# Order of the scores, the second halves' turns and the exponentials in the two loops of sparse attention pairs

## The reference

```
s = q @ k.T * 0.125           # 512 x 512, only keys up to the query count
s = where(mask, s, -1e30)
p = softmax(s)                # NSA: times its gate
y = p @ v
```

## Time and profile before

| | |
|---|---|
| device time, three runs | 2798.03, 2798.65, 2803.75 us, median 2798.65 |
| the profiled execution's own time | 2803.71 us |
| its span in the profile | 2801.9 us |
| busy: PE, DVE, ACT, POOL | 2664.3 us (95%), 1644.3 us (59%), 1143.0 us (41%), 117.6 us (4%) |
| mean granted clock of TensorE | 0.985 |
| DSA's loop of pairs | about 1419 to 1498 us of the span |
| NSA's loop of pairs | about 1680 to 1831 us of the span |

### The profile page before, as it was taken

The page is one execution under the profiler, slowest core; times in us unless marked ns, Lnnn a source line. Parts: engine busy times, 40 slices in busy tenths (PEclk is TensorE's granted clock), DMA queues, the critical chain, the costliest instruction groups (busy, mean ns, idle before and its releaser), DMA issues.

```text
span 2801.9 us, 38810 instructions
## 1 busy us (share of the span) xinstructions
PE 2664.3 (95%) x13931; PEld 2138.0 (76%) x13931; DVE 1644.3 (59%) x3050; ACT 1143.0 (41%) x1988; POOL 117.6 (4%) x104
## 2 busy tenths in 40 slices
PE   7999999999999999999979988999999989999998
PEld 5567888888887888887856875577777768788887
DVE  6235725547876844637874267755677775563551
ACT  4444322236764322225364318822455552332221
POOL 0000000000000000001300010000111110000000
PEclk9999999999999999999999989999999999999999
DMA  4112333322222233332201310022222213433331
GB/s 143 46 54 67 105 98 97 99 83 68 75 81 77 76 105 97 98 98 83 76 16 46 99 38 1 1 83 83 83 68 68 68 53 98 129 91 103 90 101 64
DMA packets 59684, 217.82 MB, mean 78 GB/s; under 512 B 6432, under 2 KB 6560, under 8 KB 59424
## 3 DMA queue, kind: packets, MB, share of 16 engines
q1 hardware_dynamic: 57920, 209.76, 24.5%
q0 software_dynamic: 1632, 6.29, 0.7%
HBM read 211.83 MB, written 4.19 MB: 77 GB/s over the span
## 4 chain that ended last, share of the span: by engine, by line
PE 75%; DVE 13%; DVEq 4%; ACT 4%; issue 3%; ACTq 0%; DMA 0%; POOL 0%; SPq 0%
PE ps L385 21%; PE ps L387 21%; PE ps L386 21%; DVE work L2141 1%; PE ps L526 1%; DVE ring_lo L325 1%; DVE big L3377 1%; PE ps L777 1%; DVEq L3435 1%; DVE work L2160 1%; DVE work L2484 1%; PE ps L2066 1%; DVEq L2487 1%; DVE ps L2475 1%; ACT ring_hi L318 1%
## 5 line engine op out<-in xcount | busy, mean ns | idle before, releaser
L385 PE MATMUL ps<-a_hi,ring_hi 128*128 128x512 f32 (+1 forms) x1896 | 750.6, 396 | 34.9 <-DVE ring_lo L325 19.4
L387 PE MATMUL ps<-a_hi,ring_lo 128*128 128x512 f32 (+1 forms) x1912 | 742.0, 388 | 0.0
L325 DVE TENSOR_TENSOR ring_lo<-ring,ring_hi 128x1024 fp32r<-128x1024 f32 x358 | 437.8, 1224 | 484.4 <-ACT ring_hi L318 454.4
L386 PE MATMUL ps<-a_lo,ring_hi 128*128 128x512 f32 (+1 forms) x1832 | 710.8, 388 | 0.0
L318 ACT ACTIVATE ring_hi<-ring 128x1024 fp32r<-128x1024 f32 x376 | 395.5, 1055 | 498.4 <-PE ps L387 498.3
L385 PEld LDWEIGHTS ps<-a_hi,ring_hi 128*128 128x128 f32 x1896 | 358.5, 189 | 122.3 <-DVE ring_lo L325 18.3
L387 PEld LDWEIGHTS ps<-a_hi,ring_lo 128*128 128x128 f32 x1912 | 361.1, 189 | 74.9
L386 PEld LDWEIGHTS ps<-a_lo,ring_hi 128*128 128x128 f32 x1832 | 346.1, 189 | 68.4 <-issue 1.0
L386 PE MATMUL ps<-hid_lo,ring_hi 128*128 128x512 f32 (+1 forms) x992 | 380.6, 384 | 0.0
L385 PE MATMUL ps<-hid_hi,ring_hi 128*128 128x512 f32 (+1 forms) x928 | 354.6, 382 | 0.0
L387 PE MATMUL ps<-hid_hi,ring_lo 128*128 128x512 f32 (+1 forms) x928 | 354.2, 382 | 0.0
(11 more groups left out here) (450 smaller groups left out, 3343.2 us busy)
## 6 DMA issues: line engine op xcount, KB each, us to landing
ring<-weights SPq DMA_DIRECT2D x392, 512.0 KB, 3.6
h<-x SPq DMA_DIRECT2D x1, 2048.0 KB, 9.2
residual<-h POOLq DMA_DIRECT2D x4, 512.0 KB, 3.4
h<-residual POOLq DMA_DIRECT2D x1, 2048.0 KB, 11.4
out<-h POOLq DMA_DIRECT2D x1, 2048.0 KB, 7.9
tab<-tables SPq DMA_DIRECT2D x1, 1648.0 KB, 15.4
big<-positions SPq DMA_DIRECT2D x1, 256.0 KB, 3.4
col<-columns SPq DMA_DIRECT2D x1, 164.5 KB, 4.1
```

The source lines that it names most:

```text
L325: dve.tensor_tensor(lo, M.ring[:, b % RING, :], hi.bitcast(F32), ALU.subtract).then_inc(M.sem("blocks_split"), 1)
L385: pe.matmul(out, w_hi, hi, start=start, stop=False)
L386: pe.matmul(out, w_hi, lo, start=False, stop=False)
L387: return pe.matmul(out, w_lo, hi, start=False, stop=stop)
```

## The change

Three orders are changed, each by moving one step, and one wait is added so that no buffer is written before it is read. The work of each engine is the same.

```diff
@@ pe, body
                 turn(i, n, 0)
                 if n or not isinstance(i, int) or i:
                     out(i, n - 1)
-                turn(i, n, 1)
                 if n + 2 < per or nxt:
                     scores(i, n + 2)
+                turn(i, n, 1)
@@ act, body
                 keep(i, n, 0)
                 if n + 1 < per or nxt:
                     exp(i, n + 1, 0)
-                keep(i, n, 1)
                 if n or not isinstance(i, int) or i:
                     finish(i, n - 1)
                 if n + 1 < per or nxt:
                     exp(i, n + 1, 1)
+                keep(i, n, 1)
@@ dve, mask
-            dve.wait_ge(M.sem(f"{A}_scores"), i * per + (n + 1))
+            if half == 0 or (isinstance(i, int) and i == 0 and n < 2):
+                dve.wait_ge(M.sem(f"{A}_scores"), i * per + (n + 1))
+            else:
+                dve.wait_ge(M.sem(f"{A}_turned"), i * (6 * per) + 6 * (n - 1))
```

## The result

The new order is slightly slower (by 0.2%): median 2804.78 us (2802.62 to 2810.07, 10 runs) against 2798.47 (2797.34 to 2803.75, 10 runs) beside it, ratio 1.0022 with a 95% interval of 1.0012 to 1.0032, which is 3.4 to 9.0 us. The forecast's +4.6 lies in it; the bound of 0.2% (5.6 us) does too, so the measurement doesn't decide between the forecast's band, "within 0.2%", and "slower by more".

The account below looks back on a forecast made before the run. No engine had slack: TensorE was busiest, ScalarE nearly as tight, the chain through VectorE third. 0.8 + 1.96 - 0.5 + 0.5 + 1.8 = +4.6 us on the median 2798.65 gave 2803.3; range 2796.5 to 2811.

Parts of the forecast that it names:

- the forecast's band: Whole kernel: slower by +1.5 to +5.6 us; chance 0.36.
- Start, 0: Start of each loop: S(2) and S(3) stay where they were, 0 us; TensorE owes one turn.
- these prices: Both ends of both loops: slowdowns from TensorE's lower clock stay unchanged, as waits are of similar or greater length.
- Steady, +0.8 and +0.5: Steady steps: neighbouring turns and keeps add +0.20 four times in DSA, +0.09 six times in NSA.
- ScalarE's round of 8.35: Steady step: ScalarE's work sums to 8.35, more than TensorE's 8.22, so ScalarE sets the step.
- End, +1.96 and +1.8: Loop ends: T1(6) and T1(14) wait for a ScalarE copy; O(6) +1.96 in DSA, X +1.8 in NSA.
- The gain of O(7): End of DSA: O(7) no longer waits for F(6), only for the late K1(7); -0.5 us.
- The added wait, 0: VectorE's new wait before M1(n): T1(n-2) ends before M1(n) starts, so it costs 0.
- A: Steady steps: neighbouring turns let TensorE's clock fall, 48 us in some 22 steps, 2851; chance 0.04.
- B: Steady steps: if M1 comes late, E1, K1, both turns and out slide; 2806 to 2812; chance 0.32.
- C: Turns: waits for the first copy partly go in neighbouring turns, 10 us off, 2793; chance 0.12.
- D: The lower clock falls into the new idle time and costs less; up to -6 us, 2797; chance 0.16.

Follow-up runs that it names:

- e3: Changed kernel, but ScalarE keeps the old order in each loop's last step with an exponential; 2805.89 us, 1.0024 of the kernel before.
- e7: Changed kernel with one more 128x512 copy on ScalarE ahead of each finish of DSA; 2813.49 us, one execution.
- e8: Kernel before with one more 128x512 copy on ScalarE ahead of each finish of DSA; 2805.55 us, one execution.
- e1: Changed kernel, but step 0 of each loop keeps the old order on TensorE and ScalarE; 2801.10 us, 1.0009 of the kernel before.
- e4: Changed kernel with the old order in step 0 and in the last step with an exponential; 2802.29 us, 1.0010 of the kernel before.
- the filled pair: Kernel before and changed kernel, each with idle matmuls in TensorE's long waits at both loops' starts and ends; 2794.61 us and 2797.22 us.
- e2: Changed kernel with six idle matmuls ahead of S(2) in each loop; 2800.72 us, 1.0004 of the kernel before.
- e9: Kernel before with three idle matmuls ahead of T1(0) in each loop; 2796.18 us, 0.9987 of the kernel before.

## Why the prediction was right in sum, and where its steps failed

**In sum:** forecast 2803.3, measured 2804.78; +4.6 reckoned, +5.0 by the loops of the profiles, +6.3 by the medians (3.4 to 9.0). Part of the agreement is luck, as the steps show.

**Start, 0: S(2)'s place right, the price wrong.** "It starts at the same time and TensorE stands idle" held to the hundredth (7.93 in both). S(3) didn't stay where it was: +1.41 and +1.59. The step that failed is the last one on the clock, "so I take these prices as unchanged". A wait of 3.78 in place of 1.8 let the clock fall earlier, and S(2) took 4.56 instead of 3.33; in NSA 4.57 instead of 3.62, and T1(0) behind it was slower too. The size isn't fixed: S(2) took 3.80 to 4.58 with the new order at the start (after, e3, e7, both loops) and 3.26 to 4.01 with the old (before, e8, e1, e4). With the clock held the same stretch is only 0.17 to 0.19 longer.

**Steady, +0.8 and +0.5: size near (+0.67 and +0.33), cause wrong.** The step named was ScalarE's round of 8.35 "so that ScalarE sets the step". Two of its terms were off. An exponential is 2.18 from its start to the next work when nothing waits (E1(7) at 1484.46, K1(6) at 1486.64); my 2.32 took in 0.14 of waiting for a turn. And K1 to K0 is 1.95 (1478.44 to 1480.39), not 1.83. That gives 1.95 + 1.41 + 2 x 2.18 + 0.48 = 8.20, and 8.33 was measured; the extra copy shows the 0.13 between them. The step is TensorE's: T1 to O takes 3.67 as one block (1477.74 to 1481.41), two turns apart took 3.50 (8.16 less 2.31 for out and 2.35 for scores). Within the block a third short wait for a bank comes to the two of 0.25 and 0.31 that the rows show; it can't be seen as one, since it lies inside the row of 10. In NSA the price is hidden in part: the two waits of the scores for VectorE (0.44 at 1729.71 and 0.39 at 1764.44 of before) are gone, and those two steps are 0.68 shorter, the other ten together 1.01 longer.

**End, +1.96 and +1.8: mechanism right, sizes off.** The wait in the middle of T1(6) for L2102 is there (2.46 against "2.8"), behind F(5) and E1(7) as worked out. O(6) came 14.92 after S(7), not 14.40, for the reason left out: T0(7) ran at the lower clock (0.52). With the clock held it is 14.19. The gain of O(7) was 0.58 against 0.5. The debt of a turn from the start is paid here, as T1(5) and K1(5) now stand behind S(7).

**The clock at the ends, "unchanged": in this pair of executions it gave something back, which is luck.** O(6) took 2.49 instead of 3.50, X and O(14) 3.57 instead of 5.91. Against the filled pair, stretch by stretch, the change costs 2.6 us of clock at the starts ((10.47 - 8.26) - (9.06 - 8.09) = 1.24 in DSA, 1.40 in NSA) and gets 2.4 back at the ends (+0.96 up to O(6) and X, -3.36 behind them): 5.0 with the clock, 4.8 without. That is how a sum with no change of the clock in it came out near. The 2.4 isn't a gain of the order. With the same new end, from the last S to the next product took 22.76, 24.19 and 22.94 in DSA (after, e1, e2) and 23.04, 24.25, 22.73 and 23.08 in NSA (and e7); with the old end 21.87 and 20.43 in DSA (before, e9) and 22.91, 21.61 and 21.41 in NSA (and e8). The means differ by 2.2 and 1.3, 3.4 in all, about what the filled pair has (1.43 and 1.99). This pair had only +0.89 in DSA and +0.13 in NSA there (-1.59 + 2.48, -2.34 + 2.47), 2.4 less. So the profiles' 5.0 is more likely low than high, which fits the medians (+6.3).

**The added wait, 0:** in the waits of after no row names a turn as what VectorE waited for. VectorE's order is the same before and after, so only two orders are changed, those of TensorE and ScalarE. No kernel has the wait alone.

**The rivals.** A fell: 25 us of steady steps with neighbouring turns had the granted clock at 1.00, and so had the block of T1(5) and T0(6) taken alone (1477.74 to 1481.41). The Trainium skill (TensorE: Matmul & The Clock Gate, Part 4: PE-mode transpose) says that transposes don't count as work towards the full clock. These rows show that 3.67 us of them in a step of 8.33, with out and scores around them, don't lower it; they don't settle whether transposes count, and next to a wait of 2.46 us turns did have 0.52. B's condition didn't come about: no exponential slid. C fell: the waits inside turns became one more per pair, not fewer. D isn't shown: the ends of this one pair looked like it, those of the other kernels don't.

## What to carry to other kernels

When a step moves behind another engine's queue, draw the first and the last rounds of the loop apart from the steady one: here 3.8 of the 4.8 us with the clock held lie there, 3.4 of them behind the last scores. A step that no longer runs in the shadow of a wait at the start isn't lost there, but it is still to be done when the last scores are through, and its copy with it. Take an engine's own round from rows with no wait in them, and where the slack lies in the round, not only its sum. And price TensorE's clock together with each wait: a few idle matmuls in the waits at the start and the end of each loop made the kernel before faster (2794.06 us, 0.9984 of it), more than any order did; the version with a third fill (2794.61 us) is equal to it within the intervals.

## What was unexpected of the hardware

TensorE's clock answers to waits of a few us, and the price falls on what comes next. After 3.78 us idle the next 4.56 us ran at 0.50; after 2.46 idle the turns had 0.52 and the out behind them 0.92; with six idle matmuls and 1.19 us of waiting S(2) had the full clock. A wait doesn't always show in its own window: in the kernel with only the end in the old order the 5.75 us with the wait of 2.31 had a granted clock of 1.00, and O(6) behind it 0.57. What a wait costs differs from one kernel to the next even where order and waits are the same. The kernel before with fills at the start alone (e9) has the same waits at the end of DSA as before, 1.05 and 1.46 us, and its timeline of TensorE there is

```profile
1485.97 0.44 PE L2047 MATMUL ps<-tab,work 128*128 128x128 f32 x2 [1.46 <-ACT big L2104]
1486.34 2.37 PE L2066 MATMUL ps<-big 128*64 128x512 f32 x16
```

where before's O(6) took 3.57. With the new end O(6) took 2.56 in after and 3.97 with the start in the old order (e1). With fills the stretches agree: S(2) to S(3) of NSA was 8.96 in all three kernels with the old order and fills. I have no run that shows what decides where the fall lands; one execution alone therefore can't price a wait.
